# Router pieces in another order beside the output projection, and the top 64 of 512 found as the top 64 of two halves, merged by one elementwise maximum

## The reference

```python
def expert_choice_ffn(h, w_router, w_gate, w_up, w_down):
    cap = max(1, EC_CAPACITY * t // N_EXPERTS)      # 64 of 512 latents, 32 of 256 context tokens
    aff = jax.nn.softmax((h @ w_router).astype(F32), axis=-1)      # 16 experts
    gate, idx = lax.top_k(jnp.swapaxes(aff, 1, 2), cap)
    xs = jax.vmap(lambda hb, ib: hb[ib])(h, idx)
    hid = jax.nn.silu(jnp.einsum('becd,edf->becf', xs, w_gate)) * jnp.einsum('becd,edf->becf', xs, w_up)
    y = jnp.einsum('becf,efd->becd', hid, w_down) * gate[..., None].astype(h.dtype)
```

## Time and profile before

| what | value |
|---|---|
| median of 3 runs | 2403.15 us (2401.86 to 2405.89) |
| the profiled execution | 2401.48 us |
| its span | 2399.7 us |
| busy: PE, DVE, ACT, POOL | 88%, 32%, 19%, 5% |
| mean granted TensorE clock | 0.935 |
| HBM | 228 GB/s over the span |

### The profile page before, as it was taken

The page is one execution under the profiler, slowest core; times in us unless marked ns, Lnnn a source line. Parts: engine busy times, 40 slices in busy tenths (PEclk is TensorE's granted clock), DMA queues, the critical chain, the costliest instruction groups (busy, mean ns, idle before and its releaser), DMA issues.

```text
span 2399.7 us, 33292 instructions
## 1 busy us (share of the span) xinstructions
PE 2119.6 (88%) x13904; PEld 1077.9 (45%) x13904; DVE 765.0 (32%) x1425; ACT 449.1 (19%) x1020; POOL 121.2 (5%) x119
## 2 busy tenths in 40 slices
PE   5998999628698859999999998999998499999997
PEld 3544656428694323333333334554674144444442
DVE  2144523597873251010011113000772511111113
ACT  2223421665311010000000002000551000000001
POOL 0000000211110000111111000000000000000000
PEclk8999999857588979999999999999999699999999
DMA  7229720141134139999999983110313299999996
GB/s 283 71 90 350 247 96 10 38 132 45 71 118 174 53 127 379 391 397 387 395 399 396 403 332 107 54 43 12 103 37 150 114 382 421 421 421 421 421 421 278
DMA packets 110620, 551.32 MB, mean 230 GB/s; under 512 B 13025, under 2 KB 25825, under 8 KB 61329
## 3 DMA queue, kind: packets, MB, share of 16 engines
q1 hardware_dynamic: 102512, 522.29, 55.2%
q0 software_dynamic: 7168, 23.83, 3.5%
q10 hardware_dynamic: 800, 3.15, 0.3%
HBM read 525.27 MB, written 22.38 MB: 228 GB/s over the span
## 4 chain that ended last, share of the span: by engine, by line
PE 74%; DMA 11%; DVE 10%; ACT 2%; issue 2%; SPq 1%; POOL 0%; DVEq 0%; POOLq 0%; ACTq 0%
PE ps L2258 22%; PE ps L2270 5%; PE ps L508 4%; DMA ring_sb<-expert_w_up 4%; PE ps L1798 4%; PE ps L911 3%; DMA work_sb<-expert_w_up 3%; PE ps L2628 3%; PE ps L1832 2%; PE ps L2600 2%; PE ps L2609 2%; PE ps L2288 2%; DMA ring_sb<-ada_w 2%; PE ps L2308 2%; PE ps L910 2%
## 5 line engine op out<-in xcount | busy, mean ns | idle before, releaser
L2258 PE MATMUL ps<-work_sb 128*32 128x512 f32 (+1 forms) x2432 | 411.4, 597 | 12.3 <-DMA work_sb<-expert_w_up 6.2
L2258 PE MATMUL ps<-ring_sb,work_sb 128*32 128x512 f32 (+1 forms) x2048 | 300.9, 600 | 12.8 <-DMA ring_sb<-expert_w_up 8.2
L2258 PEld LDWEIGHTS ps<-work_sb 128*32 128x32 f32 (+1 forms) x2432 | 123.7, 120 | 237.0 <-issue 229.6
L2258 PEld LDWEIGHTS ps<-ring_sb,work_sb 128*32 128x32 f32 (+1 forms) x2048 | 87.4, 118 | 201.7 <-issue 195.0
L2449 DVE TENSOR_TENSOR work_sb<-ps,work_sb 128x512 f32<-128x512 f32 x32 | 20.6, 687 | 440.0 <-PE ps L2270 331.0
L2380 ACT ACTIVATE work_sb<-ps 128x1024 f32<-128x1024 f32 x16 | 16.4, 1024 | 514.8 <-PE ps L2270 294.0
L508 PE MATMUL ps<-ring_sb,work_sb 128*128 128x512 f32 (+1 forms) x288 | 106.4, 531 | 0.9 <-DVE work_sb L403 0.9
L2270 PE MATMUL ps<-work_sb 128*32 128x512 f32 x768 | 101.5, 597 | 0.0
L2270 PE MATMUL ps<-ring_sb,work_sb 128*32 128x512 f32 x768 | 100.8, 596 | 0.0
L911 PE MATMUL ps<-work_sb,ring_sb 128*128 128x512 f32 x192 | 98.0, 592 | 0.0
L2468 DVE SCALAR_TENSOR_TENSOR work_sb<-ps,work_sb,gates_sb 128x1024 f32<-128x1024 f32 x16 | 20.5, 1284 | 232.8 <-PE ps L2270 124.8
(11 more groups left out here) (424 smaller groups left out, 2926.2 us busy)
## 6 DMA issues: line engine op xcount, KB each, us to landing
work_sb<-expert_w_down SPq DMA_DIRECT2D x88, 1024.0 KB, 18.6
work_sb<-expert_w_gate SPq DMA_DIRECT2D x64, 1024.0 KB, 7.6
ring_sb<-expert_w_gate SPq DMA_DIRECT2D x64, 1024.0 KB, 10.4
ring_sb<-expert_w_up SPq DMA_DIRECT2D x64, 1024.0 KB, 14.9
work_sb<-expert_w_up SPq DMA_DIRECT2D x56, 1024.0 KB, 14.5
ring_sb<-ada_w SPq DMA_DIRECT2D x96, 512.0 KB, 5.6
ring_sb<-expert_w_down SPq DMA_DIRECT2D x32, 1024.0 KB, 13.9
ring_sb<-wout SPq DMA_DIRECT2D x16, 512.0 KB, 5.9
```

Source lines behind the costliest of these rows:

```text
L2258: mm = pe.matmul(ps[g:g + wide, bank + n, :], lat_src[:, k, g:g + wide], us[e][:, n * 512:(n + 1) * 512], start=(k == 0), stop=(k == KT - 1))
```

## The change

The copies of line 2005 and the sums of 2016 move ahead by one product in DVE's list, so they stand behind the product at whose end their input is ready. The last product is cut in two on PE, and the logits of the tile before the last and the lower half of the last tile's turn stand in the gap. The last tile's upper half is copied by DVE, its `XM` rows are made after the softmax, and POOL issues the load of `WR` ahead of that of `x`. The choice works on rows of 256: partitions 0 to 15 have latents 0 to 255, 64 to 79 latents 256 to 511, and 32 to 47 the context. Each half gives its 64 largest in falling order; the second list is read backwards, and the elementwise larger of the two lists is the top 64 of both. Seven instructions on 16 partitions do the merge.

```diff
@@ outproj0_pe, then outproj_pe
                 if j < 4:
                     half_products(j, range(4, KT))
+                elif j < 2 * NT - 1:
+                    pe.wait_ge(op_ok, j - 3)
+                    half_products(j, turned + list(range(4, KT)))
                 else:
                     pe.wait_ge(op_ok, j - 3)
-                    half_products(j, turned + list(range(4, KT)))
+                    half_products(j, turned)
+                    route_within_pe(pe, 0)
+                    half_products(j, range(4, KT))
                 route_beside_pe(pe, 0, j)
...
                 for k in range(KT):
+                    if j == 2 * len(tiles) - 1 and k == 4:
+                        route_within_pe(pe, 1)
@@ outproj_dve
-                if j % 2 == 0 and j >= 4:
-                    route_sums_dve(dve, l, j // 2 - 2)
-                if j % 2 == 1 and j >= 5:
-                    route_logits_dve(dve, l, (j - 5) // 2)
-                if j % 2 == 1 and j >= 3:
-                    route_dve(dve, l, (j - 3) // 2)
-            last = len(tiles) - 1
-            route_sums_dve(dve, l, last - 1)
-            route_dve(dve, l, last)
+                if j >= 4 and j % 2 == 0:
+                    route_logits_dve(dve, l, j // 2 - 2)
+                if j >= 2 and j % 2 == 0:
+                    route_low_dve(dve, l, j // 2 - 1)
+                    route_root_dve(dve, l, j // 2 - 1)
+                    route_rows_dve(dve, l, j // 2 - 1)
+                if 3 <= j < n - 1 and j % 2 == 1:
+                    route_sums_dve(dve, l, (j - 3) // 2)
+                if j == n - 2:
+                    route_sums_dve(dve, l, last - 1)
+                    route_low_dve(dve, l, last)
             route_logits_dve(dve, l, last - 1)
+            route_high_dve(dve, l, last)
+            route_root_dve(dve, l, last)
             route_sums_dve(dve, l, last)
             route_logits_dve(dve, l, last)
@@ route_within_pe, route_end_pe
+        def route_within_pe(pe, l):
+            last = len(routed_tiles(l)) - 1
+            route_logits_pe(pe, l, last - 1)
+            route_turn_pe(pe, l, last, (0,))
         def route_end_pe(pe, l):
             last = len(routed_tiles(l)) - 1
             route_back_pe(pe, l, last - 1)
-            route_turn_pe(pe, l, last)
-            route_logits_pe(pe, l, last)
+            route_logits_pe(pe, l, last, (0,))
+            route_turn_pe(pe, l, last, (1,))
+            route_logits_pe(pe, l, last, (1,))
             route_back_pe(pe, l, last)
@@ route_act
-                act.wait_ge(rt_mm, 2 * (NT * l + n) + 2)
...
+                if n < len(routed_tiles(l)) - 1:
+                    act.wait_ge(rt_mm, 2 * (NT * l + n) + 2)
...
@@ router_weights_dve
-                nc.vector.memset(ROWS0[0:rows, :], -1.0)
-                nc.vector.memset(TOPS[0:rows, :], 0.0)
-                nc.vector.memset(PICKF[0:rows, :], 0.0)
-                nc.vector.memset(AFFC[:, :, 0:C0], 0.0)
+                nc.vector.memset(PICKF[0:C0 + NE, :], 0.0)
+                nc.vector.memset(AFFQ, 0.0)
@@ route_dve
-        def route_dve(dve, l, n):
+        def route_low_dve(dve, l, n):
...
+        def route_high_dve(dve, l, n):
+
+            dve.wait_ge(rt_mm, 2 * (NT * l + n) + 2)
+            nc.vector.tensor_copy(RT[:, 4:8, :].rearrange("p k t -> p (k t)"), ps[:, TURN_BANKS[l][1], :]).then_inc(rt_hi, 1)
...
@@ pick_pe
-            for tt in tiles_of(l):
-                if tt < CT:
-                    tr = pe.transpose(ps[0:C0 + NE, 6, tt * P:(tt + 1) * P], AFFC[:, tt, :], IDENT)
-                else:
-                    tr = pe.transpose(ps[0:NE, 5, (tt - CT) * P:(tt - CT + 1) * P], AFF[:, tt, :], IDENT)
+            for c in range(2):
+                tr = pe.transpose(ps[0:GROUPED, 5, c * P:(c + 1) * P], AFFQ[:, c, 0:GROUPED], IDENT)
@@ pick_dve (GROUPED = 80, B0 = 64, HALF_L = 256)
                                     ALU.mult).then_inc(mo["aff"], 1)
+            route_rows_dve(dve, l, n - 1)
             dve.wait_ge(mo["aft"], l + 1)
-            if l == 0:
-                nc.vector.tensor_copy(ROWS0[C0:C0 + NE, 0:CTX], ps[C0:C0 + NE, 6, 0:CTX])
-            step(nc.vector.tensor_copy(ROWS0[0:NE, :], ps[0:NE, 5, 0:LAT]))
+            step(nc.vector.tensor_copy(ROWS0[0:GROUPED, :], ps[0:GROUPED, 5, 0:HALF_L]))
             for r in range(CAP_L // 8):
-                some = slice(0, rows if r < CAP_C // 8 else NE)
-                row, top, pick = ROWS0[some, :], TOPS[some, 8 * r:8 * r + 8], PICKU[some, 8 * r:8 * r + 8]
+                row, top, pick = ROWS0[0:GROUPED, :], TOPS[0:GROUPED, 8 * r:8 * r + 8], PICKU[0:GROUPED, 8 * r:8 * r + 8]
                 step(nc.vector.max(top, row))
...
             step(last)
+            tops, picks = TOPS[0:NE, 0:CAP_L], PICKU[0:NE, 0:CAP_L]
+            nc.vector.tensor_copy(OTHER, downwards(TOPS[B0:B0 + NE, 0:CAP_L]))
+            step(nc.vector.tensor_scalar(OTHER_ID, downwards(PICKU[B0:B0 + NE, 0:CAP_L]), float(HALF_L), None, ALU.add))
+            nc.vector.tensor_tensor(LARGER, tops, OTHER, ALU.is_ge)
+            step(nc.vector.tensor_tensor(PICKF[0:NE, 0:CAP_L], picks, OTHER_ID, ALU.subtract))
+            nc.vector.tensor_tensor(TOPS[0:NE, CAP_L:2 * CAP_L], tops, OTHER, ALU.max)
+            step(nc.vector.tensor_tensor(LARGER, LARGER, PICKF[0:NE, 0:CAP_L], ALU.mult))
+            nc.vector.scalar_tensor_tensor(PICKF[0:NE, :].rearrange("p (e s) -> p e s", e=2),
...
-            nc.vector.tensor_copy(TOPS[0:NE, CAP_L:2 * CAP_L], TOPS[0:NE, 0:CAP_L]).then_inc(mo["sid"], 1)
-            twice = bc(PICKU[0:NE, :].unsqueeze(1), [NE, 2, CAP_L])
-            nc.vector.tensor_scalar(PICKF[0:NE, :].rearrange("p (e s) -> p e s", e=2), twice, float(CTX), None, ALU.add) \
-                .then_inc(mo["sid"], 1)
+            nc.vector.tensor_copy(TOPS[0:NE, 0:CAP_L], TOPS[0:NE, CAP_L:2 * CAP_L]).then_inc(mo["sid"], 1)
@@ gpsimd block
+            pool.wait_ge(dn_ok, len(ORDER))
+            pool.dma_start(WR, t["router"][0].rearrange("p (k e) -> p k e", k=KT)).then_inc(mo["wr"], 16)
             pool.wait_ge(yt_tr, NT)
             pool.dma_start(H[:, CT:NT, :], t["x"].rearrange("(t p) d -> p t d", p=P)).then_inc(h_late, 16)
-            pool.wait_ge(dn_ok, len(ORDER))
             pool.dma_start(SEL1, t["sel"].rearrange("p (s m) -> p s m", s=8)).then_inc(ada1_in, 16)
-            pool.dma_start(WR, t["router"][0].rearrange("p (k e) -> p k e", k=KT)).then_inc(mo["wr"], 16)
```

More of the change, by code:

```diff
@@ L1842, in outproj_dve @@
             tiles, base = routed_tiles(l), OP0 * l
-            n = 2 * len(tiles)
+            n, last = 2 * len(tiles), len(tiles) - 1
             for j in range(n):
@@ L1894, in route_turn_pe @@
             if n > 0:
-                pe.wait_ge(rt_dve, NT * l + n)
-                pe.wait_ge(rt_act, NT * l + n)
-            for k in range(KT):
-                tr = pe.transpose(ps[:, TURN_BANKS[l][k // 4], k % 4 * P:(k % 4 + 1) * P], H[:, tt, cols(k)], IDENT)
-                if k % 4 == 3:
-                    tr.then_inc(rt_mm, 1)
+                pe.wait_ge(rt_lo, NT * l + n)
+                pe.wait_ge(rt_hi, NT * l + n)
+            for half in halves:
+                for k in range(4):
+                    tr = pe.transpose(ps[:, TURN_BANKS[l][half], k * P:(k + 1) * P], H[:, tt, cols(4 * half + k)], IDENT)
+                tr.then_inc(rt_mm, 1)
         def route_shift_pe(pe, l):
@@ L1918, in route_spread_pe, with route_logits_pe @@
             mm.then_inc(rl_mm, 1)
[L1920 removed]
+        def route_logits_pe(pe, l, n, halves=(0, 1)):
             tt = routed_tiles(l)[n]
@@ L1924, in route_logits_pe @@
                 pe.wait_ge(rl_ok, logits_ok(l, 2 * n + 1))
-            for half in range(2):
-                pe.wait_ge((rt_dve, rt_act)[half], NT * l + n + 1)
+            for half in halves:
+                pe.wait_ge((rt_lo, rt_hi)[half], NT * l + n + 1)
                 for j in range(4):
@@ L2111, in pick_dve @@
             t0, n = tiles_of(l)[0], len(tiles_of(l))
-            rows = C0 + NE if l == 0 else NE
             lg = AFF[:, t0:, :]
```

45 lines of the change are left out of this document (27 added, 18 removed).

## The result

The changed kernel takes 2349.6 us (median of 4 runs, 2344.2 to 2354.42) against 2404.45 for the kernel before (4 runs): a ratio of 0.9772, 95% interval 0.9748 to 0.9797. The forecast was 2354, its range 2347 to 2370. The profiled execution took 2348.14 us, with a span of 2346.3.

A forecast was written before the change was run, and what follows sets the result against it. PE is three quarters of the chain, waiting for DVE beside the projections and idle during the choice of tokens. Terms sum to 48.7 us off the profiled 2401.5, giving 2352.8 and a median near 2354; range 2347 to 2370.

The forecast's parts named there:

- the granted clock: Beside the projections: PE falls to 1.2 GHz behind waits; without them 4.5 us of at most 5.0 come back.
- Waits beside the projections and the router weights: PE's waits for DVE's copies go except in the tail, 24.2 us; layer 0's wait for router weights goes, 3.5 us.
- The tail: Last product's gate to softmax: two `XM`, copies and turn work leave the path, 2.5 us per layer, 5.0 in all.
- Turn and copy of the affinities: Softmax to first MAX8: `XM` lies over two transposes, then one 256-column copy; 1.6 and 0.6, 2.2 us gained.
- The rounds: Choice of tokens: 23 instructions per layer read rows of 256 instead of 512, 6.0 us each, 12.0 gained.
- The merge: Choice of tokens: seven added instructions less one that goes cost 1.2 us in each layer, -2.4 us.
- What follows later than before: Layer 1: later `XM` store and expert weights touch the first gather for a moment, -0.3 us.
- new waits: Rival beside projections and tail: new waits eat a third of the reordering and most of the clock's gain, 2368; chance 0.16.
- slower: Rival in the projections: denser PE is granted less clock, products run at 1.2 GHz, up to 2494; chance 0.02.
- the gather collides: Rival in layer 1: first gather meets the late weights in full, 6.3 us more, 2360; chance 0.08.
- layer 1 keeps its end: Rival: layer 1's weight stream isn't held by PE's start, so its 15.7 us are lost, 2370; chance 0.04.

The follow-up runs named there:

- uncut product: Changed kernel with the last product of each projection left whole, logits and turn behind it, moved copies and `XM` as changed: 2350.2 us, ratio 0.9783.
- router load alone: Kernel before with one edit, the load of layer 0's router weights issued ahead of that of `x`: 2397.03 us, ratio 0.9968.
- each half of the change alone: Kernel before with only the new choice of tokens: 2388.43 us; changed kernel with the old choice on rows of 512: 2359.19 us.
- early `XM`: Changed kernel with the last tile's `XM` made ahead of the last sums again, as before the change: 2352.23 us, ratio 0.9792.
- late choice: Changed kernel with 20 further MAX8, each waited for, ahead of the rounds in layer 1 alone: 2359.34 us, ratio 0.9800.
- choice only: Kernel before with the new choice of tokens alone (rows of 256, merge, two turns of 80 columns): 2388.43 us, ratio 0.9931.

## Why the prediction was right, step by step

It was right in sign and mechanism, and near in size: 2354 forecast, 2349.6 measured, 48.7 us won by the sum and 54.5 by the marks. Of the 5.8 us between them about half is one term that was too small, the granted clock, and half is a gain behind the choice that had no term and is luck.

*Waits beside the projections and the router weights*, 24.2 + 3.5. Right. Inside P0 of the kernel before PE waits 9.4 + 6.9 us for the copies, as shown above, and 3.5 before line 1909; inside P1:

```profile
PE ps L1931 <- DVE work_sb L2005: 4.2, 2, 2.6
PE ps L1937 <- DVE work_sb L2016: 3.5, 2, 1.8
```

Together that is 27.5 us, and all of it is gone.

*The tail*, 5.0. Right in the sum, wrong in its parts. T fell by 3.88 and 3.52, and the cut put 1.25 into each last product: 4.9. But the uncut product keeps the whole of the gain, so the pieces inside the product are not its source. Most of it, 1.95 us in each layer, is that the last tile's turn starts earlier, since the logits ahead of it no longer wait for the copy of line 2005. What the rest is made of (the upper half's copy on DVE, the sums, the clock in the tail) no run takes apart. Of the two `XM` of 0.75 that I took off the path in each layer the last tile's was hidden (0.25 and 0.02 us when put back); the other was not tried.

*Turn and copy of the affinities*, 2.2. Right: 1.53 + 0.63 (4.45 less 2.75 is 1.7 for layer 0, where I wrote 1.6). *The rounds*, 12.0. Right: a MAX8 takes 424 ns on 256 columns and 80 partitions, the copy's duration as assumed, and the rounds 10.58 us. *The merge*, -2.4. Right: C fell by 4.76 and 4.85, together 9.6 = 12.0 - 2.4. The backward copy took 0.18, as a forward one does.

*The granted clock*, 4.5. Mis-sized, the one step that was. P0 and P1 fell by 32.5, and with the 2.5 of the cut that is 35.0; less 27.5 of waits 7.5 are left, nearly all of it the clock (6.9 by the windows set on the gate). My bound of 5.0 was none: falls reach into the next window, and I had listed one of each. Of the Trainium skill's rule (TensorE: Matmul & The Clock Gate, HAM oscillation) the trace agrees that falls go with gaps, as filling them showed, and that the time lost is half of the time at the lower clock, for shortfall times window gives 1.7 us a fall and the marks 1.4 to 1.6. It does not show a fall behind each gap that comes again: only four of 13 had one, and in the page's own case the waits are longer than the 1.6 to 2.6 us of these. By the rule I should have taken all that the windows held.

*Behind the choice*, no term. I had looked at the projections alone, and that 1.00 stands where PE had no gap is not so behind layer 1's small products, where the kernel before has 0.59 with PE busy throughout. The fall there gave 1.7 of `end`, and the time from first product to first freed slot, which starts at 1.2 GHz, went from 6.68 to 5.39: 3.0 more. This is luck: the router load alone gave the same 3.0 (5.22 and an `end` of 478.63) without touching these stretches, and each half of the change alone a still shorter `end`.

*What follows later than before*, -0.3. Measured 0. PE waited 5.51 us for the gather of layer 1 and 5.56 before. The gather's packets began at 1855.1, 1.7 us behind its issue, and the last of the weights' ended at 1855.8, so both moved for 0.7 us, and PE waited no longer. Where the Trainium skill says that transfers of all issuers interleave on the same engines (DMA: Bandwidth & Descriptors, Issuing engines are not separate DMA queues), nothing here speaks against it; the two lay side by side for too short to cost.

The sum by the marks: 27.5 + 7.5 + 4.9 + 2.2 + 12.0 - 2.4 + 3.0 - 0.1 (layer 0's experts and the gathers) = 54.6.

Of the rivals, *new waits* and *slower* are refuted by the waits and by 1.00 in every window of P0 and P1; *the gather collides* by the early `XM`; *layer 1 keeps its end* by the late choice.

What stays open: which gap makes the clock fall and which doesn't. Of the 13 gaps in P0 and P1 of the kernel before four are followed by a fall; the same program repeats its falls, and an edit far away moves them (P0 100.83 with the choice only). Behind layer 1's small products not even the same program always repeats its fall.
